# A two-layer encoder: DeltaNet chunk matrices stacked in 64 columns, and logits, tables and state outputs of the state-space part in another form

## What is computed

```
y = real(einsum(states, c)) + d * u                       # S5, states by a scan over time
kk = einsum('bhntd,bhnjd->bhntj', k, k)                   # 64 x 64 for each chunk and head
lower = eye(64) + beta * kk * decay_strict
sol = triangular_solve(lower, [beta * v, beta * gamma * k])
u_new, w_k = split(sol)
qk = einsum('bhntd,bhnjd->bhntj', q, k) * decay_causal
w = u_c - wk_c @ state;  o = qg_c @ state + qk_c @ w;  state = dec_c * state + kt_c.T @ w     # chunk after chunk
```

## Time and profile before

| | us |
|---|---|
| median of 3 runs | 1858.15 |
| lowest, highest | 1855.84, 1859.2 |
| profiled execution | 1858.16 |
| its span | 1856.3 |
| busy in the span: TensorE | 1716.1 (92%) |
| VectorE | 820.3 (44%) |
| ScalarE | 625.7 (34%) |
| POOL | 243.0 (13%) |

### The profile page before, as it was taken

How to read it: one execution, slowest core, us unless ns; L and a number is a source line. 1 busy time by engine, 2 the same in 40 slices (tenths; PEclk the granted TensorE clock), 3 DMA queues, 4 the chain that set the end, 5 groups by cost and what they waited for, 6 DMA issues and landing times.

```text
span 1856.3 us, 20717 instructions
## 1 busy us (share of the span) xinstructions
PE 1716.1 (92%) x8408; PEld 1413.4 (76%) x8408; DVE 820.3 (44%) x1064; ACT 625.7 (34%) x1004; POOL 243.0 (13%) x301
## 2 busy tenths in 40 slices
PE   6998585999998999999999999789998999999999
PEld 5877565987776788888888888447885878888887
DVE  5753644444535244443322543883445343444212
ACT  5323044223544243222211433663534242332111
POOL 1781103430100011111100000000000011111000
PEclk9997677999999999999999999899999999999999
DMA  6305001012331133333223232122520223333321
GB/s 202 92 23 114 1 1 46 1 69 67 138 114 46 46 90 92 91 103 101 91 91 106 86 104 91 46 69 68 181 91 23 69 69 108 94 90 95 109 91 68
DMA packets 146794, 151.96 MB, mean 82 GB/s; under 512 B 8864, under 2 KB 109344, under 8 KB 146592
## 3 DMA queue, kind: packets, MB, share of 16 engines
q1 hardware_dynamic: 146720, 150.92, 26.5%
HBM read 147.76 MB, written 3.15 MB: 81 GB/s over the span
## 4 chain that ended last, share of the span: by engine, by line
PE 84%; DVE 9%; ACT 4%; issue 2%; DMA 0%; POOL 0%; SPq 0%; ACTq 0%; DVEq 0%
PE ps L317 23%; PE ps L318 23%; PE ps L319 23%; PE ps L1521 2%; PE ps L1544 2%; PE ps L1158 1%; PE ps L1168 1%; PE ps L1878 1%; PE ps L934 1%; PE ps L1173 1%; PE ps L875 1%; DVE sb L1948 1%; PE ps L777 1%; PE ps L876 1%; ACT w_hi L285 1%
## 5 line engine op out<-in xcount | busy, mean ns | idle before, releaser
L317 PE MATMUL ps<-h_hi,w_hi 128*128 128x512 f32 x864 | 338.4, 392 | 7.2 <-DVE w_lo L1692 3.9
L318 PE MATMUL ps<-h_lo,w_hi 128*128 128x512 f32 x864 | 337.4, 391 | 0.0
L289 DVE TENSOR_TENSOR w_lo<-raw,w_hi 128x2048 fp32r<-128x2048 f32 x70 | 160.5, 2293 | 395.3 <-ACT w_hi L285 395.3
L285 ACT ACTIVATE w_hi<-raw 128x2048 fp32r<-128x2048 f32 x84 | 160.8, 1915 | 421.6 <-PE ps L319 420.5
L319 PE MATMUL ps<-h_hi,w_lo 128*128 128x512 f32 x704 | 274.5, 390 | 0.0
L317 PEld LDWEIGHTS ps<-h_hi,w_hi 128*128 128x128 f32 x864 | 162.9, 189 | 42.1 <-issue 4.7
L318 PEld LDWEIGHTS ps<-h_lo,w_hi 128*128 128x128 f32 x864 | 163.1, 189 | 33.6
L1692 DVE TENSOR_TENSOR w_lo<-raw,w_hi 128x2048 fp32r<-128x2048 f32 x44 | 138.1, 3138 | 53.5 <-ACT w_hi L1674 53.5
L319 PEld LDWEIGHTS ps<-h_hi,w_lo 128*128 128x128 f32 x704 | 132.5, 188 | 27.7
L317 PE MATMUL ps<-w_hi,a_hi 128*128 128x512 f32 x352 | 137.3, 390 | 1.7 <-DVE up L1690 1.7
L1674 ACT ACTIVATE w_hi<-raw 128x2048 fp32r<-128x2048 f32 x44 | 84.3, 1916 | 161.1 <-PE ps L319 161.1
(11 more groups left out here) (354 smaller groups left out, 2849.1 us busy)
## 6 DMA issues: line engine op xcount, KB each, us to landing
raw<-in_f_w_gate SPq DMA_DIRECT2D x44, 512.0 KB, 4.0
raw<-in_f_w_up SPq DMA_DIRECT2D x44, 512.0 KB, 5.2
raw<-in_f_w_down SPq DMA_DIRECT2D x44, 512.0 KB, 4.4
raw<-in_xa_w_kv SPq DMA_DIRECT2D x16, 1024.0 KB, 5.0
raw<-in_c_w_qkv SPq DMA_DIRECT2D x12, 1024.0 KB, 5.1
raw<-in_ab_w_in SPq DMA_DIRECT2D x10, 1024.0 KB, 5.4
raw<-in_xa_w_q SPq DMA_DIRECT2D x8, 1024.0 KB, 5.1
raw<-in_xa_w_out SPq DMA_DIRECT2D x8, 1024.0 KB, 5.0
```

The costliest lines, as they stand in the source:

```text
L285: a.activation(w_hi[:, n % 2, :], raw[n % 2], ACT.Copy).then_inc(sem("w_hi"), 1)
L289: v.tensor_tensor(w_lo(n)[:, n % 2, :], raw[n % 2], w_hi[:, n % 2, :].bitcast(F32), ALU.subtract).then_inc(sem("w_lo"), 1)
L317: pe.matmul(out, a[0], b[0], start=start, stop=False)
L318: pe.matmul(out, a[0], b[1], start=False, stop=False)
```

## The change

The two 64 x 64 blocks of a tile are stacked: chunk 0 in partitions 0 to 63, chunk 1 in 64 to 127, each in the same 64 columns. So masks, A, U, T, Y, QK and the decays have 4 x 64 instead of 4 x 128 columns per tile. Each 128 x 128 matmul on them becomes two matmuls of 64 x 64 with 64 columns, one on array rows and columns 0 to 63, the next on 64 to 127; both write the same bank, in different partitions. The transposes ahead of the solve become such matmuls against a stacked identity. `uw` is split in the same way into four banks per tile, so its third tile waits for the first tile's copies, and ScalarE copies two halves per tile.

In the S5 part the logits make the weights stationary (16 columns) and stream 512 frames; VectorE copies the 16 rows, and TensorE turns them after the third group of table transposes. L777 has 128 columns; the padding of K8 (4 x 112 columns) is cleared instead of that of G. The second part of the state outputs goes through the two partition halves in turn, and ScalarE copies banks 0 to 3, VectorE 4 to 7.

```diff
-CON = {n: i * P for i, n in enumerate(["ident", "inc", "neg", "m1", "m2", "m3", "m4", "m5", "m6", "same", "first", "second"])}
-N_CON = len(CON) * P
+CON = {n: i * P for i, n in enumerate(["ident", "same", "first", "second"])}
+CON.update({n: 4 * P + i * CHUNK for i, n in enumerate(["inc", "neg", "m1", "m2", "m3", "m4", "m5", "m6", "one"])})
+N_CON = 4 * P + 9 * CHUNK
...
+                   "logit_rows": ("s5_dt", 1), "logit_turned": ("s5_rd", 1),
...
+            for k in range(KT):
+                for part in range(2):
+                    ins = pe.matmul(ps[0:4 * GH, 7, :], w_ab_split[:, k, :, :].rearrange("p a b -> p (a b)"), hT0[part][:, k, :],
+                                    start=(k == 0 and part == 0), stop=(k == KT - 1 and part == 1))
+            ins.then_inc(sem("logit_mm"), 1)
+
+        def logits_turn_pe(pe):
+            pe.wait_ge(sem("logit_rows"), after("logit_rows", 1))
             for i in range(TT):
-                for k in range(KT):
-                    for part in range(2):
-                        ins = pe.matmul(ps[:, 7, i * 16:(i + 1) * 16], hT0[part][:, k, i * P:(i + 1) * P],
-                                        w_ab_split[:, k, :, :].rearrange("p a b -> p (a b)"), start=(k == 0 and part == 0), stop=(k == KT - 1 and part == 1))
-            ins.then_inc(sem("logit_mm"), 1)
+                ins = pe.transpose(ps[:, 7, i * 4 * GH:(i + 1) * 4 * GH], logit_rows[:, i * P:(i + 1) * P], ident[0:4 * GH, 0:4 * GH])
+            ins.then_inc(sem("logit_turned"), 1)
...
             if n == 3:
-                v.memset(G[:, :, 8:15, :], 0.0).then_inc(sem("s5_g"), 1)
+                v.wait_ge(sem("s5_g"), 4)
+                v.memset(K8[:, :, 8 * S5_CH:], 0.0).then_inc(sem("s5_g"), 1)
...
-                            ins = pe.matmul(bank[:, o * 240:(o + 1) * 240], C_pad[:, g, :], G[:, g, :, :].rearrange("p m c -> p (m c)"),
+                            ins = pe.matmul(bank[:, o * P:(o + 1) * P], C_pad[:, g, :], G[:, g, 0:8, :].rearrange("p m c -> p (m c)"),
                                             start=(r == 0), stop=(r == 7))
                 ins.then_inc(sem("s5_tab"), 1)
+                if s == 2:
+                    logits_turn_pe(pe)
...
-            for n in range(S5_G):
-                gp, g2, o = place(n)
-                r = slice(g2 * 64, g2 * 64 + 64)
-                pe.matmul(o, t_c[r, gp, :], V_re[r, gp, :, :].rearrange("p i c -> p (i c)"), start=False, stop=False, skip_group_check=True)
-                ins = pe.matmul(o, z_re[r, gp, :], V_im[r, gp, :, :].rearrange("p i c -> p (i c)"), start=False, stop=True, skip_group_check=True)
+            for gp in range(S5_GP):
+                for g2 in range(2):
+                    _, _, o = place(gp + S5_GP * g2)
+                    r = slice(g2 * 64, g2 * 64 + 64)
+                    pe.matmul(o, t_c[r, gp, :], V_re[r, gp, :, :].rearrange("p i c -> p (i c)"), start=False, stop=False, skip_group_check=True)
+                for g2 in range(2):
+                    _, _, o = place(gp + S5_GP * g2)
+                    r = slice(g2 * 64, g2 * 64 + 64)
+                    ins = pe.matmul(o, z_re[r, gp, :], V_im[r, gp, :, :].rearrange("p i c -> p (i c)"), start=False, stop=True, skip_group_check=True)
                 if gp % 4 == 3:
                     ins.then_inc(sem("s5_y"), 1)
...
-            for b in range(0, 8, 2):
+            for b in range(4):
...
-                v.tensor_copy(*s5_y_evac(v, b)).then_inc(sem("y_v"), 1)
+                v.tensor_copy(*s5_y_evac(v, 4 + b)).then_inc(sem("y_v"), 1)
         def s5_back_pe(pe):
             for f in range(4):
-                pe.wait_ge(sem(("y_a", "y_v")[f % 2]), after(("y_a", "y_v")[f % 2], 3 + f // 2))
+                pe.wait_ge(sem("y_a"), after("y_a", f + 1))
+                pe.wait_ge(sem("y_v"), after("y_v", f + 1))
...
-        A_T, QK_T = gd(TT, GH, P), gd(TT, GH, P)
-        U_m, T_m, Y_m, A_l = gd(TT, GH, P), gd(TT, GH, P), gd(TT, GH, P), gd(TT, GH, P)
+        A_T, Y_m, QK_T = gd(TT, GH, CHUNK), gd(TT, GH, CHUNK), gd(TT, GH, CHUNK)
+        U_m, T_m, A_l = gd(TT, GH, CHUNK), gd(TT, GH, CHUNK), gd(TT, GH, CHUNK)
+        o_sq = reg(arena + 18432, TT, GH, GD)
+        k_sq = o_sq[:, 0:2]
...
+        def logits_rows_dve(v):
+            v.wait_ge(sem("logit_mm"), 1)
+            v.tensor_copy(logit_rows, ps[0:4 * GH, 7, :]).then_inc(sem("logit_rows"), 1)
+
         def logits_dve(v):
-            v.wait_ge(sem("logit_mm"), 1)
+            v.wait_ge(sem("logit_turned"), after("logit_turned", 1))
...
-            for n, m in enumerate(("inc", "same", "first", "second")):
-                ins = pe.matmul(ps[:, 7, 16 * n:16 * n + 16], ccol(m), g, start=True, stop=True)
+            for r in CHUNKS:
+                pe.matmul(ps[r, 7, 0:16], ccol("inc")[r], g[r], start=True, stop=True)
+            for n, m in enumerate(("same", "first", "second")):
+                ins = pe.matmul(ps[:, 7, 16 * (n + 1):16 * (n + 2)], ccol(m), g, start=True, stop=True)
...
-            for bank, l, r in ((7, k_nT, k_bT), (3, k_nT, q_nT)):
+            for bank, left, right in ((7, k_nT, k_bT), (3, k_nT, q_nT)):
                 for h in range(GH):
-                    ins = pe.matmul(ps[:, bank, h * P:(h + 1) * P], l[:, h, :], r[:, h, :], start=True, stop=True)
+                    for r in CHUNKS:
+                        ins = pe.matmul(ps[r, bank, h * CHUNK:(h + 1) * CHUNK], left[:, h, r], right[:, h, r], start=True, stop=True)
                 ins.then_inc(sem("g_prod"), 1)
             pe.wait_ge(sem("g_bc"), i + 1)
             for h in range(GH):
-                ins = pe.matmul(ps[:, 4, h * P:(h + 1) * P], g_bc[:, h, :], ccol("inc"), start=True, stop=True)
+                for r in CHUNKS:
+                    ins = pe.matmul(ps[r, 4, h * CHUNK:(h + 1) * CHUNK], g_bc[r, h, r], ccol("inc")[r], start=True, stop=True)
...
-                v.scalar_tensor_tensor(dec_m[:, h, :], ps[:, 4, h * P:(h + 1) * P], gs["gc"][:, i, h:h + 1],
+                v.scalar_tensor_tensor(dec_m[:, h, :], ps[:, 4, h * CHUNK:(h + 1) * CHUNK], gs["gc"][:, i, h:h + 1],
                                             ccol("neg"), ALU.subtract, ALU.add).then_inc(sem("g_diff"), 1)
...
-                v.tensor_tensor(dst[:, i], ps[:, bank, :].rearrange("p (a b) -> p a b", a=GH), dec_m, ALU.mult).then_inc(sem("g_at"), 1)
-
+                v.tensor_tensor(dst[:, i], ps[:, bank, 0:SOLVE_W].rearrange("p (a b) -> p a b", a=GH), dec_m, ALU.mult).then_inc(sem("g_at"), 1)
...
-                g.tensor_tensor(U_m[:, i], bc(ident, 1, GH), U_m[:, i], ALU.subtract).then_inc(sem("g_u"), 1)
+                g.tensor_tensor(U_m[:, i], bc(ccol("one"), 1, GH), U_m[:, i], ALU.subtract).then_inc(sem("g_u"), 1)
...
-                    ins = pe.transpose(ps[:, i % 2, h * P:(h + 1) * P], U_m[:, i, h, :], ident)
+                    for r in CHUNKS:
+                        ins = pe.matmul(ps[r, i % 2, h * CHUNK:(h + 1) * CHUNK], U_m[r, i, h, :], ccol("one")[r], start=True, stop=True)
                 ins.then_inc(sem("sv_tr"), 1)
...
-                        ins = pe.matmul(ps[:, n % 2, h * P:(h + 1) * P], A_l[:, i, h, :], T_m[:, i, h, :], start=True, stop=True)
+                        for r in CHUNKS:
+                            ins = pe.matmul(ps[r, n % 2, h * CHUNK:(h + 1) * CHUNK], A_l[r, i, h, :], T_m[r, i, h, :], start=True, stop=True)
...
-                        ins = pe.matmul(ps[:, 2 + n % 3, h * P:(h + 1) * P], Y_m[:, i, h, :], U_m[:, i, h, :], start=True, stop=True)
+                        for r in CHUNKS:
+                            ins = pe.matmul(ps[r, 2 + n % 3, h * CHUNK:(h + 1) * CHUNK], Y_m[r, i, h, :], U_m[r, i, h, :], start=True, stop=True)
                     if l < LEVELS - 1:
                         if n >= 3:
                             pe.wait_ge(sem("sv_t"), n - 2)
                         for h in range(GH):
-                            ins = pe.matmul(ps[:, 5 + n % 3, h * P:(h + 1) * P], U_m[:, i, h, :], Y_m[:, i, h, :], start=True, stop=True)
+                            for r in CHUNKS:
+                                ins = pe.matmul(ps[r, 5 + n % 3, h * CHUNK:(h + 1) * CHUNK], U_m[r, i, h, :], Y_m[r, i, h, :], start=True, stop=True)
                     ins.then_inc(sem("sv_d"), 1)
...
-                a.activation(flat3(Y_m[:, n % TT]), ps[:, n % 2, :], ACT.Copy).then_inc(sem("sv_yc"), 1)
+                a.activation(flat3(Y_m[:, n % TT]), ps[:, n % 2, 0:SOLVE_W], ACT.Copy).then_inc(sem("sv_yc"), 1)
...
-                v.tensor_tensor(flat3(U_m[:, i]), flat3(U_m[:, i]), ps[:, 2 + n % 3, :], ALU.subtract).then_inc(sem("sv_u"), 1)
+                v.tensor_tensor(flat3(U_m[:, i]), flat3(U_m[:, i]), ps[:, 2 + n % 3, 0:SOLVE_W], ALU.subtract).then_inc(sem("sv_u"), 1)
                 if n < (LEVELS - 1) * TT:
-                    v.tensor_tensor(flat3(T_m[:, i]), flat3(T_m[:, i]), ps[:, 5 + n % 3, :], ALU.subtract).then_inc(sem("sv_t"), 1)
```

(52 more changed lines are left out.)

18 lines of the change are left out of this document (11 added, 7 removed).

## The result

The changed kernel takes **1794.96 us** (median of 4 runs, 1794.4 to 1796.58) beside 1856.99 (4 runs, 1854.85 to 1859.2): ratio 0.9667, 95% interval 0.9651 to 0.9684, or 62 us less. That is 2 us above the forecast and inside the range. The profiled execution took 1794.4 us, with a span of 1792.5.

The account below looks back on a forecast made before the run. TensorE was taken as busy 92% of the span, at reduced clock around 140 to 325 us, where the change falls. Terms summing to -65.1 us from 1858.16 gave 1793 us; range 1783 to 1829, the forecast's own 1785 to 1804.

Parts of the forecast that it names:

- The two steps that carry the sum: The two largest terms: state outputs, -17.8 us, and solve, -23.6 us, both from pairs of quarter-array matmuls overlapping.
- zeroing: Clearing 448 instead of 3584 columns starts the weight split earlier and removes a half-clock stretch on TensorE: -4.2 us.
- logits: Sixteen 512-column matmuls replace 64 with 16 columns, plus a copy and small transposes; first reader earlier: -3.4 us.
- states: VectorE chain between the tables and the state outputs: not touched, only moves, 0 us.
- behind the outputs: The 7.4 us after the state outputs, before at clock 0.50: -1.5 us, bounds 0 to -3.
- transposes: Transposes ahead of the solve become pairs of plain matmuls, 32 x 107 ns at half clock: -0.3 us.
- State outputs: Second part of the state outputs: pairs on different row halves overlap, clock rises after 3.7 us; 26.7 to 8.9 us, -17.8.
- Solve: Groups of eight paired matmuls take 0.47 us instead of 0.90, levels 5.8 instead of 10.84, at full clock: -23.6 us.
- Both rivals of that step: Solve: clock stays 1.2 GHz in pairs (1827 us, chance 0.12); pairs sharing a bank run serially (1816 or 1876, 0.05 each).
- Behind the solve: From solve to recurrence, 8.3 to 6.2 us, ScalarE's two half copies per tile setting the pace: -2.0 us.
- Tables: Table products (L777) with 128 instead of 240 columns, 32 matmuls in 7.2 instead of 13.32 us: -6.4 us.
- Tiles: Gated DeltaNet tiles: 256-column steps cheaper on VectorE and ScalarE, POOL masks halved, last products shorter: -5.9 us, bounds -4.5 and -7.5.

Follow-up runs that it names:

- e_outputs_blocks: Changed kernel with the second part of the state outputs, its copies and waits in the old order, one partition half after the other: 1817.13 us, ratio 0.9778.
- e_uw_blocks: Changed kernel with the products behind the solve issued half by half, so neighbours use the same rows: 1798.63 us, ratio 0.971.
- e_tables_back: Changed kernel with G's padding cleared again and the table product back at 240 columns: 1806.42 us, ratio 0.9729.
- e_warm_gdn: Changed kernel plus unused 128 x 512 matmuls on TensorE behind each DeltaNet tile's products: 1790.1 us, ratio 0.9644.
- e_warm_all: Changed kernel plus unused matmuls ahead of the state outputs, behind each DeltaNet tile's products and ahead of the table products: 1787.36 us, ratio 0.9631.
- e_warm_x: `e_warm_all` with the load of x moved behind the memory load and the first chunk of the recurrence: 1786.4 us, ratio 0.9625.

## Why the prediction was right, and where its steps were not

The two steps that carry the sum held. That the result lies only 2 us from the forecast is in part luck: up to the recurrence five steps gave 4.6 us more than forecast (zeroing, logits, states, behind the outputs, transposes), the other five 8.9 less. The range that the prediction calls its own is also added up wrongly: its bounds, summed, give 1788 to 1810 and not 1785 to 1804. **State outputs**: pairs overlap and the clock rises inside; I had put the rise at 3.7 us by L869, and it came at 5.7, which costs 2.0 x 0.5 = 1.0 us, the whole difference. `e_outputs_blocks` shows one quarter at a time at 0.50 to the end, with TensorE never waiting for a copy. **Solve**: a group takes 0.47 us as forecast, at clock 1.00. Of the 2.4 us that are missing, 1.2 lie in the first three groups, which still ran at 0.50 (0.86 each); I had let the solve start at full clock behind transposes that I had myself put at half clock. Another 0.7 are the pauses of TensorE in the first two levels, and the rest is spread over the levels; even the third and fourth, without such a pause, took 6.22 and 5.94 us instead of 5.8:

```profile
294.84 0.38 PE L1211 MATMUL ps<-sb 64*64 64x64 f32 x5 [0.50 <-issue]
...
303.10 0.22 PE L1194 MATMUL ps<-sb 64*64 64x64 f32 x1
...
309.04 2.38 PE L1194 MATMUL ps<-sb 64*64 64x64 f32 x64
```

Both rivals of that step are out: the clock is 1.00 in the window below, and records of the two quarters stand in one bank 29 ns apart. The Trainium skill (TensorEngine Tiling (Array Packing), Restrictions and Gotchas) says that different row tiles cannot access the same PSUM bank simultaneously. This case's measurement differs for quarters that lie in different rows and different columns: 16 records in 0.47 us where records on one quarter stand 55 to 60 ns apart, and the measurement decides.

Windows of the changed kernel, of the outputs before the rise, the start of the solve, and the rest of it, columns as in the earlier trace rows:

```profile
200.90:206.60 5.70, 5.64 (x54) 5.64 (x56) 0.69 (x2) 0.59 (x1) 0.00 (x0) 0.50 0.00 0
...
283.10:285.20 2.10, 2.10 (x46) 2.10 (x44) 0.00 (x0) 0.84 (x3) 0.75 (x2) 0.51 1.01 408
285.20:313.80 28.60, 27.07 (x863) 25.99 (x860) 13.70 (x36) 7.23 (x19) 10.41 (x15) 1.00 0.04 13
```

**Behind the solve** the sign was wrong: -2.0 forecast, +0.9 measured. The step that failed is the sentence "so it sets the pace" about ScalarE. I priced ScalarE's copies and never TensorE's own matmuls. They did not get shorter: L1244 streams the same 128 columns once for each half, in pairs, and L1248 streams 64 but takes as long. Eight products of 1.02 to 1.04 us, against 0.89 before, make the stage: eight times 0.13 us more. ScalarE's copies took 1.21 us a tile, near the 1.25 that I had priced, and TensorE 2.06. `e_uw_blocks` shows that TensorE bounds it. Why a product takes that much more was not tested.

**Zeroing** gave 5.2 instead of 4.2. TensorE's wait fell to 0.18 us, not 0.8. The new clear and its wait took 0.6 us, as assumed (108.74 to 109.32). But ahead of the old clear VectorE also stood idle, for 0.7 us (the step before ends at 109.20, the clear starts at 109.90), and that went with it: the clear and its wait shrank by 3.2 us and not 2.5. VectorE's table steps had also begun 0.5 us earlier (89.63 instead of 90.10); that start varies as much by itself, from 89.4 to 90.3 over the traces of the changed kernel and of those made from it. `e_tables_back` returns 5.0 us. **Tables** gave 5.3 and not 6.4 (the terms, 13.32 - 7.2 + 0.2, make 6.3). I had priced all 32 matmuls at full clock, but the clock rose only about 2 us into them (windows of the changed kernel):

```profile
153.60:155.70 2.10, 2.10 (x13) 2.10 (x12) 0.00 (x0) 0.68 (x2) 0.00 (x0) 0.56 0.98 300
155.70:161.70 6.00, 6.00 (x56) 5.95 (x54) 0.00 (x0) 0.39 (x1) 0.00 (x0) 1.00 0.64 232
```

That is 1.0 us on top of my 7.2, and 8.1 were measured. **Behind the outputs** 3.6 came instead of 1.5, and outside my bounds (0 to -3): the clock was 1.00 from 206.7 on, and it held through the transposes and up to the first tile. **Tiles** gave 4.4 instead of 5.9. Groups of the changed kernel by shape (busy us, mean ns, idle) answer:

```profile
L1230 DVE TENSOR_TENSOR sb<-sb,ps 128x256 f32<-128x256 f32 x20 | 8.4, 420 | 21.2 <-PE ps L1211 19.1 <-PE ps L1205 1.9
L1222 ACT ACTIVATE sb<-ps 128x256 f32<-128x256 f32 x20 | 7.7, 384 | 20.3 <-PE ps L1194 19.7
...
L1151 DVE TENSOR_TENSOR sb<-ps,sb 128x256 f32<-128x256 f32 x8 | 3.0, 412 | 0.5 <-ACT sb L1114 0.5
L1161 POOL TENSOR_TENSOR sb<-sb 128x256 f32<-128x256 f32 x4 | 2.9, 725 | 0.3
```

VectorE's prices were right (0.42 forecast, 420 and 412 ns) and ScalarE's high (0.44, 384). POOL's was not: half the columns cost 725 ns, not 620. And the products of the last tile took 1.8 us, not 1.4. What I had hardly looked at is the clock: `e_warm_gdn` takes 2 us off a tile with work that nobody reads, and the solve's transposes start 5.1 us earlier (275.20 against 280.30), more than the 4.4 of all the narrower steps.

**The best kernels here** are `e_warm_all` and `e_warm_x`, 0.9631 and 0.9625 of the kernel before, 7 to 8 us faster than the change alone.

## To carry to other kernels

Matmuls that use a quarter of the array should be given to TensorE so that the two row halves take turns; where one engine's narrower work makes a stage shorter, price every engine of that stage again, TensorE's weights included. An idle TensorE ahead of a dense stretch can be filled with matmuls that nobody reads, and the stage behind them runs at 2.4 GHz from its start. And when a tile is halved, look at the queue of instructions: here its packets came every 3.8 us instead of every 12.8. That a large load can hold them up is a suspicion from one trace, not shown.
